# Sixty-four of 512 tokens leave a dense expert product and are gathered by index

## The chip, the cores and the metric

The kernel runs on one core of a Trainium2 chip. The metric is the device time of one execution in microseconds, as a median over runs. The engines are named as in the profile: PE (TensorE), DVE (VectorE), ACT (ScalarE), POOL (GpSimd) and SP (SyncE, which here issues transfers only).

## The reference

A two-layer backbone over 256 latent and 256 context tokens of 1024 features. Each layer has a mixer and then a PEER block, a mixture of 16384 tiny experts of which every token uses 8 heads x 16 = 128. Layer 0 computes the block for all 512 tokens, layer 1 for the 256 latent ones. The change concerns the block alone:

```python
def peer_ffn(x, wq, keys, U, V):
    q = (x @ wq).reshape(B, L, PEER_HEADS, 2, PEER_QDIM // 2)
    s = jnp.einsum('blhpd,hpnd->blhpn', q, keys).astype(F32)
    ...                      # top 16 of each half, top 16 of their sums
    idx = e1 * N_KEYS + e2   # 128 experts of a token
    gate = jax.nn.softmax(top_s, axis=-1).astype(x.dtype)
    ...
        act = jax.nn.gelu(jnp.einsum('tkd,td->tk', U[it], xt), approximate=False) * gt
        return jnp.einsum('tk,tkd->td', act, V[it])
```

## The kernel before

The kernel computes the block densely: the activation of every expert for every token, a gate that is zero for the experts that a token did not choose, and the product with all of V. The 16384 experts are walked in 128 turns `m` of 128 experts, twice for each layer.

In the first walk (`first_products`) a turn is one product of a tile of U with all tokens: 8 chunks of the features, and for each chunk three matmuls, because a float32 value is split in a high and a low part of a narrower type (high x high, high x low, low x high). ScalarE makes the high part of the weights (`high`, w_hi), VectorE the low part (`low`, w_lo), both three turns ahead, in rings of 4; ScalarE applies the gelu, and the activations are stored to HBM (`acts_out`, one plane of 128 experts x tokens for each turn). In the same turns VectorE finds each token's experts and gates (`routing`, in slices, up to turn 53), and from turn 54 on one oct a turn (8 tokens) is turned into a dense table of gates: VectorE writes one-hot rows (`onehots`), TensorE multiplies them (`gates`, 24 small matmuls at line 828, two turns later), ScalarE stages them, and GpSimd's queue stores groups of 32 tokens to HBM (`gates_out`). With 64 octs the last one is multiplied in turn 119.

In the second walk (`second_products`) a turn is: SP loads a tile of V (512 KB), the activations of the turn (`z_load`, 256 KB) and every eighth turn a block of gates (2 MB); VectorE multiplies activation by gate (`gated`, two turns ahead), ScalarE makes the high part (`gate_high`), VectorE the low part (`gate_low`, one turn ahead); TensorE multiplies, again 8 x 3 matmuls, and adds all 128 turns up in the eight PSUM banks, one bank of 512 columns (tokens) for each 128 features. Each engine works its list strictly in order. VectorE's list is:

```python
                for m in range(NKEY):
                    if m + 2 < NKEY:
                        gated(l, m + 2)
                    if m + 1 < NKEY:
                        gate_low(l, m + 1)
                    if m + AHEAD < NKEY:
                        low(l, NKEY + m + AHEAD)
```

`high` of a turn waits until TensorE is done with the turn whose ring slot it takes, `low` waits for `high`, and SP's load of the next V tile waits for `low`. GpSimd does nothing in this walk; its queue holds the constants at the start, the stores of gates, the masks of layer 1 and the keys. Lines 555 and 876 are the matmuls of the first and the second walk, 752 those of the queries, 807 plain float32 matmuls of 128x128, 1205 `high`, 1214 `gate_high`, 1731 `low`, 1756 `gated`, 1762 `gate_low`.

Of the kernel before, what the change touches and what calls it, by code (L numbers as in the profile page):

```python
# [20 lines left out]
U32 = mybir.dt.uint32  # L21
# [4 lines left out]
P = 128  # L26
# [96 lines left out]

WIDTH = (T, SEQ)
TILES = (TT, CHUNKS)
U_BANK = (0, 1, 6, 7)
V_ORDER = (2, 3, 4, 5, 0, 1, 6, 7)

# [16 lines left out]


def octs(l):
    return WIDTH[l] // OCT


def groups(l):
    return WIDTH[l] // GTOK


EXP_TURN = [{slice_turn(l, i, AT_DIFF) + 2: i for i in range(TILES[l])} for l in range(2)]
# [24 lines left out]
def build(nc, a, out):  # L180
    with ExitStack() as ctx:
# [133 lines left out]
        I16 = iota[:, 0:TOPK]  # L315


        def weight_parts(name, hi, lo, ring):
            return [over(name + x, at, ring * TILE)[:, :].rearrange("p (r k n) -> p r k n", r=ring, k=KD)
                    for x, at in (("_w_hi", hi), ("_w_lo", lo))]  # L320
# [18 lines left out]
        def high_part(k, c, width):  # L339
# [42 lines left out]
            ck_exp ck_ready ck_t ck_in cs_ready cs_taken  # L382
            lk_exp lk_ready lk_t lk_in ls_ready ls_done
            qi_exp qi_ready lv_diff lv_exp lv_ready lv_prod lv_taken
            oi_ready osq_ready ors_ready oms_ready ostd_ready mx_ready
            f_in f_added f_tab f_normtaken dve_step lb_diff lb_exp""".split()
        S = {n: sem(n) for n in names}
        w_loaded = [sem(f"w_loaded{r}") for r in range(RING)]
        z_out = [sem(f"z_out{r}") for r in range(ZRING)]
        z_in = [sem(f"z_in{r}") for r in range(ZRING)]  # L390
        gates_out = [nc.dram_tensor(f"gates{l}", (groups(l), P, NKEY, GTOK), F32).ap() for l in range(2)]
        acts_out = [nc.dram_tensor(f"acts{l}", (NKEY, P, WIDTH[l]), F32).ap() for l in range(2)]
        block = ctx.enter_context(nc.Block())

        def parts(hi, lo, x_hi, x_lo):
# [19 lines left out]
        def _(sp):  # L415
# [40 lines left out]
            def z_load(l, m):  # L456

                r = m % ZRING
                wait(sp, S["act_ready"], l * NKEY + m - ZRING + 1)
                sp.dma_start(ZIN[:, r, 0:WIDTH[l]], acts_out[l][m]).then_inc(z_in[r], 16)  # L460

            def gates_block(l, x):

# [4 lines left out]
            def first_products(l, u, v):  # L468

                n0 = AT_PEER[l]  # L470
                for k in range(RING):
                    load(n0 + k, u[k])
                for m in range(NKEY + ZRING):
                    if m < NKEY:
                        k = m + RING
                        load(n0 + k, u[k] if k < NKEY else v[k - NKEY])
                    if l == 0 and m in LATE_TURN:
                        late(LATE_TURN[m])
                    if m == NKEY:
                        for x in range(ZRING - 1):  # L480
                            sp.wait_ge(z_out[x], 16 * (NKEY // ZRING * l + 1))
                            z_load(l, x)
                        for b in range(2):
                            sp.wait_ge(S[f"g_stored{b}"], 16 * sum(groups(x) // 2 for x in range(l + 1)))
                        for x in range(2):
                            gates_block(l, x)
                    if m >= ZRING:
                        z = m - ZRING
                        sp.wait_ge(S["gelu_done"], l * NKEY + z + 1)
                        sp.dma_start(acts_out[l][z], ZOUT[:, z % ZRING, 0:WIDTH[l]]).then_inc(z_out[z % ZRING], 16)  # L490
                for r in range(ZRING):
                    sp.wait_ge(z_out[r], 16 * (NKEY // ZRING * (l + 1)))
# [32 lines left out]
        @block.gpsimd  # L525
        def _(pool):
            for dst, src in first:
                pool.dma_start(dst, src).then_inc(S["consts_in"], 16)

            pool.wait_ge(S["w_used"], used(AT_ABOUT + N_OUT - 1))  # L530
            pool.dma_start(arena[:, 8192:10240], a["keys0"]).then_inc(S["keys_in"], 16)


            def stores(l):

                for g in range(groups(l)):
                    b = g % 2
                    pool.wait_ge(S["g_high"], 2 * l * octs(0) + 8 * (g + 1))
                    pool.dma_start(gates_out[l][g].rearrange("p e t -> p (e t)"), STG[:, b].rearrange("p e t -> p (e t)"))\
                        .then_inc(S[f"g_stored{b}"], 16)  # L540

            stores(0)
            pool.wait_ge(S["ck_exp"], 1)
            pool.dma_start(arena[:, 30752:31776], a["masks"]).then_inc(S["masks_in"], 16)
            pool.wait_ge(S["w_used"], used(AT_HGOUT + N_OUT - 1))
            pool.dma_start(arena[:, 8192:10240], a["keys1"]).then_inc(S["keys_in"], 16)
            stores(1)


        @block.tensor  # L550
        def _(pe):
# [301 lines left out]

            def value_sum(l, c):

                return ps[:, c, :] if l == 0 else ps[:, 2 + c // 2, c % 2 * SEQ:(c % 2 + 1) * SEQ]

            def second_products(l):

                n0, m0, width = AT_PEER[l] + NKEY, l * NKEY, WIDTH[l]  # L860
                pe.wait_ge(S["g_high"], 2 * sum(octs(x) for x in range(l + 1)))
                pe.wait_ge(S["slots_in"], sum(TILES[:l + 1]))
                if l == 0:
                    pe.wait_ge(S["ada_taken"], 3)

                for m in range(NKEY):
                    pe.wait_ge(S["w_used"], used(n0 + m))
                    pe.wait_ge(S["act_ready"], m0 + m + 1)
                    r, z = m % 4, m % ZRING
                    for c in V_ORDER if l == 0 and m == 0 else range(KD):  # L870
                        if m == 0 and l == 0 and c in U_BANK:
                            pe.wait_ge(S["gelu_done"], m0 + NKEY - 3 + U_BANK.index(c))
                        for n, (w, x) in enumerate(parts(WHI[:, r, c, :], WLO[:, r, c, :],
                                                         ACH[:, z, 0:width], ACL[:, z, 0:width])):

                            ins = pe.matmul(value_sum(l, c), w, x, start=m == 0 and n == 0 and (l == 0 or c % 2 == 0),  # L876
                                            stop=m == NKEY - 1 and n == 2, skip_group_check=True)
                        if m == NKEY - 1 and (l == 0 or c % 2 == 1) and c < KD - 1:
                            ins.then_inc(S["sum_done"], 1)
                    ins.then_inc(S["part_used"], 1)  # L880
# [135 lines left out]
        def _(act):  # L1016
# [169 lines left out]
            def gates_staged(l, n):  # L1186

                g, o = n // 4, l * octs(0) + n
                if n % 4 == 0:
                    wait(act, S[f"g_stored{g % 2}"], 16 * (l * groups(0) // 2 + g // 2))  # L1190
                for h in range(2):
                    act.wait_ge(S["oh_used"], 2 * o + h + 1)
                    t0 = n % 4 * OCT + 4 * h
                    copy(STG[:, g % 2, :, t0:t0 + 4], ps[:, 2 + h, :].rearrange("p (t e) -> p e t", t=4))\
                        .then_inc(S["g_high"], 1)
# [11 lines left out]

            def gate_high(l, m):

                width, r = WIDTH[l], m % ZRING  # L1210
                act.wait_ge(S["mul_ready"], l * NKEY + m + 1)
                if m >= ZRING:
                    act.wait_ge(S["part_used"], l * N_PEER + NKEY + m - ZRING + 1)
# [169 lines left out]
        def _(dve):  # L1383
# [262 lines left out]
            def routing(l, i):  # L1646
# [21 lines left out]
                for q in range(2):  # L1668
# [11 lines left out]
                step.done(dve.reciprocal(GSUM[:, 1], GSUM[:, 0]))  # L1680
                tt(GATE[:, 0], GATE[:, 0], wide(GSUM[:, 1].unsqueeze(2), [P, NH, TOPK]), ALU.mult)\
                    .then_inc(S["gates_ready"], 1)
                yield

            def routes(l):
                for i in range(TILES[l]):
                    for _ in routing(l, i):
                        yield

            def key_numbers():  # L1690
                step.done(dve.tensor_copy(KEYNUM, iota[:, :].unsqueeze(2).to_broadcast([P, P, 2])))

            def onehots(l, n):

                o, i = l * octs(0) + n, n * OCT // P
                if n * OCT % P == 0:
                    dve.wait_ge(S["slots_in"], l * TT + i + 1)
                    t = slice(i * P, (i + 1) * P)
                    dve.tensor_copy(KEY1[:, t], SL[:, 1, t])
# [3 lines left out]
                    step.done(tt(GREST, SL[:, 0, t], GHI[:, t], ALU.subtract))  # L1703
                    step.done(dve.tensor_copy(GMID[:, t], GREST))
                    step.done(tt(GLO[:, t], GREST, GMID[:, t], ALU.subtract))
                toks = slice(n * OCT, (n + 1) * OCT)

                def spread(x):
                    return x[:, toks].rearrange("p (v w) -> p v w", w=2).unsqueeze(2).to_broadcast([P, OCT // 2, NKEY, 2])
# [38 lines left out]

            def gated(l, m):

                r, b, width = m % ZRING, m // BLK % 2, WIDTH[l]
                dve.wait_ge(z_in[r], 16 * (NKEY // ZRING * l + m // ZRING + 1))
                if m % BLK == 0:
                    dve.wait_ge(S[f"g_in{b}"], 16 * (NKEY // (2 * BLK) * l + m // (2 * BLK) + 1))
# [2 lines left out]

            def gate_low(l, m):

                r, width = m % ZRING, WIDTH[l]  # L1760
                dve.wait_ge(S["acthi_ready"], l * NKEY + m + 1)
                tt(ACL[:, r, 0:width], ZIN[:, r, 0:width], ACH[:, r, 0:width], ALU.subtract)\  # L1762
                    .then_inc(S["act_ready"], 1)

            def second_products(l):
# [5 lines left out]
                for m in range(NKEY):  # L1771
# [3 lines left out]
                        gate_low(l, m + 1)  # L1775
                    if m + AHEAD < NKEY:
                        low(l, NKEY + m + AHEAD)

            def peer_residual(l):
                def ready(c):  # L1780
# [165 lines left out]
            for n in range(4, 8):  # L1946
# [131 lines left out]
```

## Time and profile before

| what | value |
|---|---|
| median of 3 runs | 3341.94 us (3341.54 to 3345.03) |
| profiled execution, span of its instructions | 3342.5 us |
| PE busy | 3169.0 us (95%) |
| DVE busy | 1942.5 us (58%) |
| ACT busy | 1222.9 us (37%) |
| POOL busy | 20.0 us (1%) |
| layer 0, second walk | from 1357 us |
| layer 1, second walk | 2941 to 3327 us |

Only the span is shown for the profiled execution, so it serves as its time. Busy time of PE counts a matmul from its first to its modelled last moment, and neighbours overlap: the mean duration of a matmul is therefore longer than the step from one to the next, and steps are read from pieces with a count (time by number) or from starts that repeat.

### The profile page before, as it was taken

The page shows a single profiled execution, that of the slowest core. Times are in us where ns is not written, and L with a number is a line of the kernel's source. Part 1 is how long each engine was busy: PE and PEld are TensorE (multiplying, and loading weights), DVE is VectorE, ACT ScalarE, POOL GpSimd, SP SyncE. Part 2 cuts the span into 40 slices and gives each one's busy share as a digit, 9 for nine tenths or more (in the row PEclk, how much of TensorE's full clock was granted, in tenths as well). Part 3 has the DMA queues.
Part 4 walks back from the last instruction along what each step waited for, and adds up shares of the span by engine and source line. Part 5 has one row for each costly group of instructions (what it writes and reads, how often), then busy time and mean ns, then how long its engine had stood idle before and what let it go on. Part 6 is the DMA issues. An engine that isn't in the chain of part 4 may idle for free.

```text
span 3342.5 us, 48135 instructions
## 1 busy us (share of the span) xinstructions
PE 3169.0 (95%) x19664; PEld 2696.4 (81%) x19664; DVE 1942.5 (58%) x3476; ACT 1222.9 (37%) x1871; POOL 20.0 (1%) x41
## 2 busy tenths in 40 slices
PE   7997889999999999999999998997789999999998
PEld 3664478888888888888888886896689999999998
DVE  5347335998555564444444444436839987656665
ACT  3313233333333333333333334325235444544444
POOL 0000000000000000000000000000000000000000
PEclk9998999999999999999999999998999999999999
DMA  5510223445666556765565552322346777787774
GB/s 204 205 60 1 73 85 98 143 144 153 229 236 221 189 189 199 240 198 195 193 199 193 193 176 70 111 76 92 116 159 200 210 254 256 252 274 260 264 262 165
DMA packets 232610, 587.91 MB, mean 176 GB/s; under 512 B 20983, under 2 KB 104008, under 8 KB 228744
## 3 DMA queue, kind: packets, MB, share of 16 engines
q1 hardware_dynamic: 227280, 528.57, 48.7%
q0 software_dynamic: 4208, 53.27, 4.1%
q8 instruction: 156, 2.56, 0.3%
q10 hardware_dynamic: 904, 3.01, 0.3%
q14 instruction: 62, 0.51, 0.0%
HBM read 483.06 MB, written 101.71 MB: 175 GB/s over the span
## 4 chain that ended last, share of the span: by engine, by line
PE 78%; DVE 14%; ACT 4%; issue 2%; DMA 1%; ACTq 0%; SPq 0%; DVEq 0%
PE ps L555 32%; PE ps L876 26%; PE ps L752 10%; PE ps L828 4%; DVE w_lo L1731 3%; PE ps L788 2%; ACT w_hi L1205 2%; PE ps L635 1%; PE ps L600 1%; DVE arena L1638 1%; DVE arena L1756 1%; DVE arena L1632 1%; PE ps L807 1%; DMA arena<-acts 1%; ACT a_t L1072 1%
## 5 line engine op out<-in xcount | busy, mean ns | idle before, releaser
L1731 DVE TENSOR_TENSOR w_lo<-wring,w_hi 128x1024 fp32r<-128x1024 f32 x512 | 626.4, 1224 | 695.3 <-ACT w_hi L1205 693.1
L555 PE MATMUL ps<-a_hi,w_hi 128*128 128x512 f32 (+1 forms) x2048 | 699.8, 342 | 9.4 <-DVE w_lo L1731 5.5
L876 PE MATMUL ps<-act_hi,w_hi 128*128 128x512 f32 (+1 forms) x2048 | 697.7, 341 | 5.2 <-DVE act_lo L1762 5.2
L555 PE MATMUL ps<-a_hi,w_lo 128*128 128x512 f32 (+1 forms) x2048 | 688.6, 336 | 0.0
L876 PE MATMUL ps<-act_lo,w_hi 128*128 128x512 f32 (+1 forms) x2048 | 688.3, 336 | 0.0
L555 PE MATMUL ps<-a_lo_q,w_hi 128*128 128x512 f32 (+1 forms) x2048 | 688.2, 336 | 0.0
L876 PE MATMUL ps<-act_hi,w_lo 128*128 128x512 f32 (+1 forms) x2048 | 687.8, 336 | 0.0
L1205 ACT CAST w_hi<-wring 128x1024 fp32r<-128x1024 f32 x512 | 533.8, 1043 | 227.7 <-PE ps L876 227.7
L555 PEld LDWEIGHTS ps<-a_hi,w_hi 128*128 128x128 f32 x2048 | 388.3, 190 | 57.0 <-DVE w_lo L1731 8.2
L876 PEld LDWEIGHTS ps<-act_hi,w_hi 128*128 128x128 f32 x2048 | 387.9, 189 | 52.7 <-issue 5.9
L555 PEld LDWEIGHTS ps<-a_hi,w_lo 128*128 128x128 f32 x2048 | 388.4, 190 | 41.0
L876 PEld LDWEIGHTS ps<-act_lo,w_hi 128*128 128x128 f32 x2048 | 388.6, 190 | 39.8
L876 PEld LDWEIGHTS ps<-act_hi,w_lo 128*128 128x128 f32 x2048 | 388.5, 190 | 39.9
L555 PEld LDWEIGHTS ps<-a_lo_q,w_hi 128*128 128x128 f32 x2048 | 388.8, 190 | 38.1
L1233 ACT ACTIVATE arena<-ps 128x512 f32<-128x512 f32 (+1 forms) x256 | 125.9, 492 | 754.4 <-PE ps L555 696.7
L1214 ACT CAST act_hi<-arena 128x512 fp32r<-128x512 f32 (+1 forms) x256 | 131.7, 515 | 456.2 <-DVE arena L1756 456.2
L1714 DVE TENSOR_TENSOR second_onehot<-key_numbers,slot_keys 128x1024 bf16<-128x1024 bf16 x96 | 66.2, 690 | 188.7 <-PE ps L828 188.7
L828 PE MATMUL ps<-gated_onehot,second_onehot 128*128 128x128 bf16 x2304 | 149.2, 219 | 0.0
L1756 DVE TENSOR_TENSOR arena<-arena 128x512 f32<-128x512 f32 (+1 forms) x256 | 141.2, 552 | 11.6 <-DMA arena<-acts 9.3
L828 PEld LDWEIGHTS ps<-gated_onehot,second_onehot 128*128 128x128 bf16 x2304 | 132.5, 97 | 18.1 <-issue 16.7
L1762 DVE TENSOR_TENSOR act_lo<-arena,act_hi 128x512 fp32r<-128x512 f32 (+1 forms) x256 | 141.4, 552 | 0.4
L555 PE MATMUL ps<-arena 128*128 128x256 f32 (+4 forms) x372 | 102.7, 427 | 12.8 <-DVE arena L1557 9.5
(253 smaller groups left out, 3448.5 us busy)
## 6 DMA issues: line engine op xcount, KB each, us to landing
wring<-in_u SPq DMA_DIRECT2D x256, 512.0 KB, 4.0
wring<-in_v SPq DMA_DIRECT2D x256, 512.0 KB, 3.7
gates<-arena POOLq DMA_DIRECT2D x24, 2048.0 KB, 8.6
wring<-in_ada SPq DMA_DIRECT2D x64, 512.0 KB, 5.5
acts<-arena SPq DMA_DIRECT2D x128, 256.0 KB, 4.4
arena<-acts SPq DMA_DIRECT2D x128, 256.0 KB, 3.4
arena<-gates SPq DMA_DIRECT2D x16, 2048.0 KB, 11.2
wring<-in_hgin SPq DMA_DIRECT2D x40, 512.0 KB, 3.4
```

The source lines that it names most:

```text
L555: ins = pe.matmul(o, l, r, start=n == 0, stop=n == len(pairs) - 1, **kw)
L752: ins = pe.matmul(o, w, x, start=c == 0 and n == 0, stop=c == KD - 1 and n == 2)
L788: ins = pe.matmul(mixed(l, c), W[:, n % RING, k, :], src[:, k, :], start=k == 0 and (l == 0 or c % 2 == 0), stop=k == KD - 1, skip_group_c ...
L828: ins = pe.matmul(ps[:, 2 + h, u * NKEY:(u + 1) * NKEY], OHB[:, n % 2, 2 * h + u // 2, :, u % 2], OHA[:, n % 2, x, 2 * h + u // 2, :, u % ...
L876: ins = pe.matmul(value_sum(l, c), w, x, start=m == 0 and n == 0 and (l == 0 or c % 2 == 0), stop=m == NKEY - 1 and n == 2, skip_group_che ...
L1205: copy(WHI[:, k % 4].rearrange("p k n -> p (k n)"), wring[:, n % RING * TILE:(n % RING + 1) * TILE])\
L1214: copy(ACH[:, r, 0:width], ZIN[:, r, 0:width]).then_inc(S["acthi_ready"], 1)
L1233: act.activation(ZOUT[:, m % ZRING, 0:WIDTH[l]], ps[:, U_BANK[m % 4], 0:WIDTH[l]], ACT.Gelu)\
L1714: tt(OHB[:, n % 2], numbers, spread(KEY2), ALU.is_equal)
L1731: tt(WLO[:, k % 4].rearrange("p k n -> p (k n)"), wring[:, n % RING * TILE:(n % RING + 1) * TILE], WHI[:, k % 4].rearrange("p k n -> p (k ...
L1756: tt(z, z, RB[l][:, b, :, m % BLK, :], ALU.mult).then_inc(S["mul_ready"], 1)
L1762: tt(ACL[:, r, 0:width], ZIN[:, r, 0:width], ACH[:, r, 0:width], ALU.subtract)\
```

## The change

For layer 0, the first 64 tokens (`PICK`) leave the second walk: its matmuls are 448 columns wide (`DENSE`), and the gates of these tokens are no longer made into a dense table, so there are 56 octs and 14 groups. The first walk still computes activations for all 512 tokens. For the 64 tokens, after the first tile's routing VectorE writes the numbers of each token's 128 experts, the addresses of their activations in `acts_out`, and the gates (`slot_numbers`), and GpSimd's queue spreads them so that a partition holds one token and one half of its 128 slots (`spread_slots`). After the first walk GpSimd fetches, for each of 64 slots k, 128 rows of V by index (`v_row`, one row of 4 KB in each partition, a ring of 4) and 128 activations by index (`words`, 4 bytes in each partition, in four batches of 16). VectorE multiplies a batch of activations with its gates and adds row times activation to an accumulator (`row_added`), one row in 1.66 turns, from turn 10 to turn 114. In turn 122 TensorE adds the accumulator, transposed and with the two halves of a token summed, into the 64 free columns of each PSUM bank (`fold`).

```diff
+PICK = (64, 0)
+DENSE = tuple(w - p for w, p in zip(WIDTH, PICK))
+SPREAD = P // PICK[0]
+QUARTER = PICK[0] // 4
+VRING = 4
+ADD_FIRST = 10
...
 def octs(l):
-    return WIDTH[l] // OCT
+    return DENSE[l] // OCT
 def groups(l):
-    return WIDTH[l] // GTOK
+    return DENSE[l] // GTOK
+def stored(l, b):
+    return sum((groups(x) + 1 - b) // 2 for x in range(l))
+def add_turn(k):
+    return ADD_FIRST + (NKEY - ADD_FIRST - 12) * k // PICK[0]
+ADD_TURN = [[k for k in range(PICK[0]) if add_turn(k) == m] for m in range(NKEY)]
+FOLD_TURN = NKEY - 6
+def pool_order():
+    first = [(oct_turn(0, 4 * g + 3) + OCT_TURNS[0] + 3, 0, g) for g in range(groups(0))]
+    return sorted(first + [(slice_turn(0, 0, SLICES - 1) + 1, 1, 0)])
...
+        VROW = [arena[:, at:at + D] for at in range(28672, 28672 + VRING * D, D)]
+        VACC = arena[:, 34560:34560 + D]
+        PSTG = hand[:, 0:3 * P].rearrange("p (q k) -> p q k", q=3)
+        PSLOT = PSTG if SPREAD == 1 else view(33920, "p (q k) -> p q k", q=3, k=PICK[0])
+        PACT = arena[:, 34112:34112 + PICK[0]]
+        FOLD = ident[:, :] if SPREAD == 1 else arena[:, 34240:34240 + PICK[0]]
+        PNUM = hand[:, 3 * P:3 * P + 1]
+        v_rows = a["v0"].rearrange("a b d -> (a b) d")
...
+        act_cells = acts_out[0].rearrange("a p t -> (a p t)").unsqueeze(1)
...
-                sp.dma_start(ZIN[:, r, 0:WIDTH[l]], acts_out[l][m]).then_inc(z_in[r], 16)
+                sp.dma_start(ZIN[:, r, 0:DENSE[l]], acts_out[l][m, :, PICK[l]:WIDTH[l]]).then_inc(z_in[r], 16)
...
-            stores(0)
+            def store(l, g):
+                b = g % 2
+                pool.wait_ge(S["g_high"], 2 * l * octs(0) + 8 * (g + 1))
+                pool.dma_start(gates_out[l][g].rearrange("p e t -> p (e t)"), STG[:, b].rearrange("p e t -> p (e t)"))\
+                    .then_inc(S[f"g_stored{b}"], 16)
+            def spread_slots():
+                n = PICK[0]
+                pool.wait_ge(S["pick_ready"], 1)
+                if SPREAD > 1:
+                    for r in range(SPREAD):
+                        pool.dma_start(PSLOT[r * n:(r + 1) * n], PSTG[0:n, :, r * n:(r + 1) * n]).then_inc(S["pick_in"], 16)
+                    pool.wait_ge(S["pick_in"], 16 * SPREAD)
+            def fetch(dst, table, q, k, sem):
+                pool.indirect_dma_start(dst, None, table, bass.IndirectOffsetOnAxis(
+                    ap=PSLOT[:, q, k:k + 1].bitcast(U32), axis=0)).then_inc(sem, 16)
+            def v_row(k):
+                wait(pool, S["row_added"], k - VRING + 1)
+                fetch(VROW[k % VRING], v_rows, 0, k, v_row_in[k % VRING])
+            def words(q):
+                for k in range(q * QUARTER, (q + 1) * QUARTER):
+                    fetch(PACT[:, k:k + 1], act_cells, 1, k, S[f"act_in{q}"])
+            def picked_rows():
+                pool.wait_ge(S["part_used"], NKEY)
+                for k in range(2):
+                    v_row(k)
+                for r in range(ZRING):
+                    pool.wait_ge(z_out[r], 16 * (NKEY // ZRING))
+                words(0)
+                for k in range(2, PICK[0]):
+                    if k % QUARTER == QUARTER // 2 and k // QUARTER < 3:
+                        words(k // QUARTER + 1)
+                    v_row(k)
+            for _, kind, g in pool_order():
+                if kind:
+                    spread_slots()
+                else:
+                    store(0, g)
+            picked_rows()
...
-                return ps[:, c, :] if l == 0 else ps[:, 2 + c // 2, c % 2 * SEQ:(c % 2 + 1) * SEQ]
+                return ps[:, c, PICK[0]:T] if l == 0 else ps[:, 2 + c // 2, c % 2 * SEQ:(c % 2 + 1) * SEQ]
+            def fold():
+                pe.wait_ge(S["fold_ready"], 1)
+                pe.wait_ge(S["row_added"], PICK[0])
+                for c in range(KD):
+                    pe.matmul(ps[:, c, 0:PICK[0]], VACC[:, c * P:(c + 1) * P], FOLD, start=False, stop=True,
+                              skip_group_check=True)
             def second_products(l):
-                n0, m0, width = AT_PEER[l] + NKEY, l * NKEY, WIDTH[l]
+                n0, m0, width = AT_PEER[l] + NKEY, l * NKEY, DENSE[l]
...
+                    if l == 0 and m == FOLD_TURN:
+                        fold()
...
-                width, r = WIDTH[l], m % ZRING
+                width, r = DENSE[l], m % ZRING
...
+                if l == 0 and i == 0:
+                    slot_numbers()
                 yield
+            def slot_numbers():
+                flat = GATE.rearrange("p q h k -> p q (h k)")
+                dve.wait_ge(S["gates_ready"], 1)
+                dve.tensor_copy(PSTG[:, 2], flat[:, 0])
+                step.done(stt(PSTG[:, 1], flat[:, 1], float(NKEY), flat[:, 2], ALU.mult, ALU.add))
+                dve.tensor_copy(PSTG[:, 0].bitcast(U32), PSTG[:, 1])
+                step.done(ts(PSTG[:, 1], PSTG[:, 1], float(T), PNUM, ALU.mult, ALU.add))
+                dve.tensor_copy(PSTG[:, 1].bitcast(U32), PSTG[:, 1]).then_inc(S["pick_ready"], 1)
...
+            def fold_matrix():
+                if SPREAD > 1:
+                    dve.tensor_reduce(FOLD, ident[:, :].rearrange("p (r t) -> p t r", r=SPREAD), AXX, ALU.add)
+                step.done(tt(PSTG[:, 0], ident[:, :], iota[:, :], ALU.mult))
+                dve.tensor_reduce(PNUM, PSTG[:, 0], AXX, ALU.add).then_inc(S["fold_ready"], 1)
+                dve.wait_ge(S["fold_ready"], 1)
+            def row_added(k):
+                if k % QUARTER == 0:
+                    q = slice(k, k + QUARTER)
+                    dve.wait_ge(S[f"act_in{k // QUARTER}"], 16 * QUARTER)
+                    step.done(tt(PACT[:, q], PACT[:, q], PSLOT[:, 2, q], ALU.mult))
+                dve.wait_ge(v_row_in[k % VRING], 16 * (k // VRING + 1))
+                if k == 0:
+                    ts(VACC, VROW[0], PACT[:, 0:1], None, ALU.mult).then_inc(S["row_added"], 1)
+                else:
+                    dve.wait_ge(S["row_added"], k)
+                    stt(VACC, VROW[k % VRING], PACT[:, k:k + 1], VACC, ALU.mult, ALU.add).then_inc(S["row_added"], 1)
...
-                o, i = l * octs(0) + n, n * OCT // P
-                if n * OCT % P == 0:
+                o, t0 = l * octs(0) + n, PICK[l] + n * OCT
+                i = t0 // P
+                if n == 0 or t0 % P == 0:
...
+                    if l == 0:
+                        for k in ADD_TURN[m]:
+                            row_added(k)
...
             query_weights(0)
+            fold_matrix()
             first_products(0)
```

## Rows read from the trace of the kernel before

**Rows 1.** The profile's page, part 1: busy time, share of the span and instructions by engine
```profile
PE 3169.0 (95%) x19664; PEld 2696.4 (81%) x19664; DVE 1942.5 (58%) x3476; ACT 1222.9 (37%) x1871; POOL 20.0 (1%) x41
```

**Rows 2.** Windows, both value stages: us, engine busy (instructions), PEclk, DMA share, GB/s
```profile
1500.00:1700.00 200.00, 200.00 (x884) 165.68 (x883) 89.62 (x111) 60.89 (x74) 0.00 (x0) 1.00 0.59 192
...
2941.00:3327.00 386.00, 383.68 (x3072) 376.23 (x3073) 240.87 (x384) 171.95 (x257) 0.00 (x0) 1.00 0.75 249
```

**Rows 3.** Waits, DVE alone, layer 0 value stage: total us, times, longest us
```profile
DVE w_lo L1731 <- ACT w_hi L1205: 369.8, 125, 3.3
DVE arena L1756 <- DMA arena<-acts: 3.8, 1, 3.8
```

**Rows 4.** Chain that ended last, 1290 to 1420 us: start us, us, what
```profile
1298.21 1.40 PE ps L828 x24
1299.61 5.54 PE ps L555 x24
...
1313.47 43.62 PE ps L555 x192
1357.09 63.01 PE ps L876 x278
```

**Rows 5.** One line (L1205), 1500 to 1560 us: durations, first and last start
```profile
L1205 ACT CAST w_hi<-wring x11: 1048/1048/1048, 1504.1 to 1558.5; 128x1024 fp32r<-128x1024 f32 x11
```

**Rows 6.** Chain that ended last, whole span: three long pieces and one repeated
```profile
455.55 65.54 PE ps L752 x288
521.84 14.54 PE ps L807 x128
...
2466.30 34.80 PE ps L752 x288
...
2699.26 5.80 PE ps L555 x48
```

**Rows 7.** Timeline around 1700 us, ACT and DVE of one turn: start us, us, what
```profile
1699.90 1.05 ACT L1205 CAST w_hi<-wring 128x1024 fp32r<-128x1024 f32 x1 [1.88 <-PE ps L876]
...
1700.98 1.23 DVE L1731 TENSOR_TENSOR w_lo<-wring,w_hi 128x1024 fp32r<-128x1024 f32 x1 [3.01 <-ACT w_hi L1205]
...
1702.12 0.69 DVE L1756 TENSOR_TENSOR arena<-arena 128x512 f32<-128x512 f32 x1
...
1702.73 0.69 DVE L1762 TENSOR_TENSOR act_lo<-arena,act_hi 128x512 fp32r<-128x512 f32 x1
```

**Rows 8.** Groups by line and shape, DVE: busy us, mean ns
```profile
L1563 DVE SCALAR_TENSOR_TENSOR arena<-arena,dskip,ps 128x512 f32<-128x512 f32 x8 | 6.0, 747 | 23.0 <-PE ps L555 23.0
```

**Rows 9.** Groups by line and shape, POOL: busy us, mean ns
```profile
L539 POOL DMA_DIRECT2D gates<-arena x24 | 12.8, 532 | 1373.2 <-ACT arena L1194 1373.2
L528 POOL DMA_DIRECT2D ident<-in_ident x1 | 0.7, 678 | 0.8 <-POOLq L2070 0.8
...
L528 POOL DMA_DIRECT2D ong<-in_ong x1 | 0.5, 534 | 0.0
...
L2070 POOL MEMSET const-float32-1.0<- 128x1 f32 x1 | 0.1, 99 | 0.0
```

**Rows 10.** DMA issues, whole span: KB each, median us from issue to landing
```profile
acts<-arena SPq DMA_DIRECT2D x128, 256.0 KB, 4.4
...
ident<-in_ident POOLq DMA_DIRECT2D x1, 64.0 KB, 4.5
...
ong<-in_ong POOLq DMA_DIRECT2D x1, 0.5 KB, 9.2
```

**Rows 11.** DMA, layer 0 value stage: packets; issues as in rows 10
```profile
DMA packets 65719, 130.37 MB, mean 189 GB/s; under 512 B 4321, under 2 KB 32993, under 8 KB 65685
...
q1 hardware_dynamic: 65685, 129.89, 57.2%
...
arena<-acts SPq DMA_DIRECT2D x125, 256.0 KB, 3.3
arena<-gates SPq DMA_DIRECT2D x14, 2048.0 KB, 11.2
```

More of the change, by code:

```diff
@@ L384, in build @@
             qi_exp qi_ready lv_diff lv_exp lv_ready lv_prod lv_taken
+            pnum_ready pick_ready pick_in act_in0 act_in1 act_in2 act_in3 pick_act row_added fold_ready
             oi_ready osq_ready ors_ready oms_ready ostd_ready mx_ready
@@ L390, in build @@
         z_in = [sem(f"z_in{r}") for r in range(ZRING)]
+        v_row_in = [sem(f"v_row_in{r}") for r in range(VRING)]
         gates_out = [nc.dram_tensor(f"gates{l}", (groups(l), P, NKEY, GTOK), F32).ap() for l in range(2)]
         acts_out = [nc.dram_tensor(f"acts{l}", (NKEY, P, WIDTH[l]), F32).ap() for l in range(2)]
+        act_cells = acts_out[0].rearrange("a p t -> (a p t)").unsqueeze(1)
         block = ctx.enter_context(nc.Block())
@@ L483, in first_products @@
                         for b in range(2):
-                            sp.wait_ge(S[f"g_stored{b}"], 16 * sum(groups(x) // 2 for x in range(l + 1)))
+                            sp.wait_ge(S[f"g_stored{b}"], 16 * stored(l + 1, b))
                         for x in range(2):
@@ L531, in _ @@
             pool.dma_start(arena[:, 8192:10240], a["keys0"]).then_inc(S["keys_in"], 16)
[L534 to L540, printed above, removed]
-            stores(0)
+            def store(l, g):
[3 more added lines that the diff above has]
+                    .then_inc(S[f"g_stored{b}"], 16)
@@ L546, in _ @@
             pool.dma_start(arena[:, 8192:10240], a["keys1"]).then_inc(S["keys_in"], 16)
-            stores(1)
+            for g in range(groups(1)):
+                store(1, g)
         @block.tensor
@@ L1189, in gates_staged @@
                 if n % 4 == 0:
-                    wait(act, S[f"g_stored{g % 2}"], 16 * (l * groups(0) // 2 + g // 2))
+                    wait(act, S[f"g_stored{g % 2}"], 16 * (stored(l, g % 2) + g // 2))
                 for h in range(2):
@@ L1705, in onehots @@
                     step.done(tt(GLO[:, t], GREST, GMID[:, t], ALU.subtract))
-                toks = slice(n * OCT, (n + 1) * OCT)
+                toks = slice(t0, t0 + OCT)
                 def spread(x):
@@ L1749, in gated @@
             def gated(l, m):
-                r, b, width = m % ZRING, m // BLK % 2, WIDTH[l]
+                r, b, width = m % ZRING, m // BLK % 2, DENSE[l]
                 dve.wait_ge(z_in[r], 16 * (NKEY // ZRING * l + m // ZRING + 1))
@@ L1758, in gate_low @@
             def gate_low(l, m):
-                r, width = m % ZRING, WIDTH[l]
+                r, width = m % ZRING, DENSE[l]
                 dve.wait_ge(S["acthi_ready"], l * NKEY + m + 1)
```

## Prediction

> **What bounds the kernel now.** The first view is the page's busy time: TensorE is busy in 95% of the span, VectorE in 58%, GpSimd in 1% [rows 1]. The share is a mean over stages, so the windows come next, for the stage that the change cuts, layer 0's value product: TensorE is busy in all of 200 us out of 200, VectorE in 90 us, ScalarE in 61, at the full granted clock (1.00, the 2.4 GHz level) [rows 2]. The waits of that stage say the same from the other side: VectorE waits 370 us in 125 turns for ScalarE's `w_hi` and 3.8 us in all for a DMA [rows 3], and `w_hi` waits for TensorE (the chain runs over TensorE alone from 1357 us on) [rows 4]. The stage is as long as its 3072 matmuls: ScalarE starts `w_hi` 11 times between 1504.1 and 1558.5 us, so a turn of 24 matmuls takes 54.4 / 10 = 5.44 us, 226.7 ns a matmul [rows 5].
>
> **The sum is made against** the profiled execution, 3342.5 us from first to last instruction, the only time shown for it; the three runs without a profile have the median 3341.94, 0.6 us away, so nothing is added. A difference under 0.2% (6.7 us) is what a measurement here can't tell from none.
>
> **Narrower products (448 columns for 512).** The trace has the same kind of matmul at two widths. 288 of them take 65.54 us with 512 columns and 34.80 us with 256 [rows 6]: 30.74 us / 288 / 256 = 0.417 ns a column, one column per cycle at 2.4 GHz, on top of a constant 14 ns. 64 columns fewer are 26.7 ns, so 200.0 ns a matmul and 4.80 us a turn; 3072 x 26.7 = **82 us** removed. Bounds: if all of 226.7 ns went with the width, 87 us; by the layer 1 pieces of 48 matmuls in 5.80 us (120.8 ns) against 226.7, 81 us [rows 5, 6]. Weight loads don't set a floor at 200 ns, because the same 128x128 loads keep up with a matmul each 120.8 ns.
>
> **Eight octs fewer.** 64 tokens less are 8 octs of gates less in the stage before (turns 112 to 119). There the chain alternates 5.54 us of product with 1.40 us of gates, and the last eight turns, without gates, take 43.62 / 8 = 5.45 us [rows 4]: 6.94 - 5.45 = 1.49 us, times 8 = **11.9 us** removed. The onehots, copies, shorter gate stores and narrower `gated`, `gate_high` and `gate_low` go too, but they hide under TensorE and count nothing.
>
> **Added on TensorE:** the fold, 8 matmuls of 128x128 by 64 columns. Plain 128x128 ones take 14.54 us / 128 = 0.11 us [rows 6]; at most 0.9 us together. It stands in turn 122 and the last row is added in turn 114, 38 us earlier.
>
> **Added on VectorE, hidden or not.** One row add is `scalar_tensor_tensor` over 1024 elements. The 512 wide one takes 0.747 us [rows 8]; 512 more cost 1.23 - 0.69 = 0.54 by the subtractions of both widths [rows 7]: 1.29 us (doubled outright, 1.49). 64 adds are 83 us, in a stage where VectorE is idle more than half of the time. What counts is the place. In the turn shown, TensorE's turn begins where ScalarE starts `w_hi` (1699.90), VectorE ends `gate_low` at 1703.42, and this activation is multiplied two turns later [rows 7]. With an add in between and turns of 4.80 us the spare is 9.6 - 3.5 - 1.3 = 4.8 us. So adds that find their row landed cost nothing, and a row late by x costs x - 4.8. `slot_numbers` and `fold_matrix` are a few short instructions: the second stands while TensorE makes queries, the first in turn 13 with weights three turns ahead; both zero, at most 1 to 2 us if that cover went.
>
> **Added on GpSimd: 128 indirect fetches,** 64 of value rows (512 KB) and 64 of activation words (128 words of 4 bytes). The trace has none, so call one fetch's time on GpSimd's queue t. Below: a direct transfer of 128 partitions is issued in 0.53 us whatever its size [rows 9]. Next: ten constants issued back to back land 4.5 (first) to 9.2 us (last) after their issue [rows 10], so the last lands 9 x 0.534 + 4.7 = 9.5 us after the first, 1.06 us each, and issue doesn't wait for landing. Above: each waits for its own landing, 4.5 us. A fetch differs from these by reading 128 indices; I take 1.1 to 1.5 us, near the rows of the same queue and partitions.
>
> How much may it be? The ring has 4 rows, and rows 8, 24 and 40 stand behind a batch of 16 word fetches that GpSimd reaches when row 3, 19 or 35 is added, 9, 8 and 9 turns before the row is due. In that go row 7's fetch, 16 words and row 8's (18t) and a landing (5 us, between 4.5 and 9.2): 18t + 5 against 9 x 4.80 - 1.3 + 4.8 = 46.7 us (8 turns: 41.9). The first batch starts some 6 us into the stage (two row fetches, then the last activations' store, 4.4 us [rows 10]) and is due in turn 10: 6 + 16t + 5 against 48 + 2.3 + 4.8 = 55.1. So **fetches are free up to t = 2.0 us** (1.8 with a landing of 9.2); past it the four stalls add to about 70t - 164 us. At 1.5 nothing; I count 0.
>
> The SBUF — State Buffer page of the Trainium skill (Who interferes with whom) says that a VectorE instruction with two SBUF inputs and a GpSimd instruction that reads SBUF shut each other out. No row here shows it; by it a fetch could wait out an add, by my estimate up to 1.3 us: t of 2.4 to 2.8 and a sum 4 to 32 us worse.
>
> **Transfers.** The stage moves 129.9 MB in 57.2% of the engines' 691 us, 48.7 engine-us a MB and 96 ns a packet [rows 11]. After: 7.8 MB less of activations and gates, 33.6 MB of rows, 8192 words at a packet each: 156 x 48.7 + 790 = 8390 engine-us, 524 of the new stage's 615 us, 85%. Layer 1's value stage runs at 75% with 99% of its time on TensorE [rows 2], and activations land in 3.3 us [rows 11] where the order of loads, three turns ahead, allows 3 x 4.80 - 1.3 = 13. I count 0, and keep some 10 us for the range.
>
> **Sum:** 3342.5 - 82.0 - 11.9 + 0.9 = 3249.5, say **3250 us**; its own range 3244 to 3260.
>
> **Rivals.**
> 1. *Fetches cost 2 to 3.6 us, since reading indices is slow or waits out adds, or the engines at 85% land them late.* The word batches then stall VectorE in turn 10 and before rows 8, 24 and 40; at 3 us 70 x 3 - 164 = 46 us come back: 3296, and between 3260 and 3335. For it: nothing shows an indirect fetch. Against: 1.06 us each in rows 9 and 10.
> 2. *Slower: GpSimd's queue becomes the bound.* From t = 3.7 us on the stalls eat the 93 us. At 4.5 us, the landing of one transfer [rows 10], 151 us come back: 3400. Against: ten transfers were issued 0.53 us apart while none had landed.
> 3. *Slower by far: GpSimd reads each index by itself.* At the shortest instruction that the trace has on it, 0.10 us [rows 9], 128 indices are 12.8 us a fetch and 128 fetches 1638 us against a stage of 615: with 11 us of start and landing and 14 turns (67 us) behind the last row, 3250 + 1101 = 4351. Against: a direct transfer, whose 128 partitions are addressed too, takes 0.53 us. The GPSIMD Engine Reference of the Trainium skill (Performance pitfalls for Q7 kernels) speaks for it: some 102 cycles for each small read command, one per gather index its example, and its Specifications give 1.2 GHz; 128 of them would be an estimated 10.9 us, and the time some 4110.
> 4. *The width gives nothing,* a floor under the matmuls at 227 ns: 3342.5 - 11.9 + 0.9 = 3332. Against it are the 120.8 ns at 256 columns.
>
> **How the numbers follow.** Forecast 0.60; rival 1 0.16; rival 2 0.13; rival 3 0.05; rival 4 0.03; and 0.03 where stall and gain meet within 0.2%. Faster is forecast, 1 and 4: 0.79; same 0.03; slower 0.18. The time is the forecast's; the range runs from the full 87 us (3244) to where rivals 1 and 4 end (3335), which holds 0.79.
>
> **What the next profile would show.** Right: `act_hi`/`w_hi` matmuls of 448 columns at a turn of 4.80 us (`w_hi` starts), the value stage at some 615 us, eight more plain turns of 5.45 us before it, VectorE's waits on row and word fetches with nothing behind them on TensorE, GpSimd's fetches at 1 to 2 us. Wrong: TensorE idle behind `act_lo` in turns 10 and around 23, 49 and 76 (rivals 1 and 2); idle in every turn (3); turns of 5.44 us (4).

## The result, and the profile after

The changed kernel takes 3264.73 us (median of 4 runs, 3264.47 to 3273.93) for 3341.9 (4 runs, 3341.54 to 3345.03): ratio 0.9773, 95% interval 0.9759 to 0.9787, **77 us faster**. The range held it, but only because it was drawn out to 3335 for rivals 1 and 4: the forecast of 3250 was 15 us too low, the forecast's own range (to 3260) missed by 5, and by the time alone it would be taken for rival 1 (3260 to 3335). The rows below show neither rival. The execution with the profile is the slowest of each four, by 9 us after and by 3 before; spans are compared with each other: 3342.5 to 3272.1, 70.4 us less.

The page and the windows answer to [rows 1, 2]. TensorE's share is what it was; in the value stage VectorE now works 121 us of 200, GpSimd 54, the transfer engines 79%, and TensorE is busy in all of it, at the full granted clock (1.00).

```profile
PE 3096.9 (95%) x19488; PEld 2688.0 (82%) x19488; DVE 1979.8 (61%) x3512; ACT 1207.7 (37%) x1855; POOL 159.5 (5%) x169
```

```profile
1500.00:1700.00 200.00, 200.00 (x970) 181.76 (x969) 121.00 (x146) 65.23 (x81) 54.00 (x50) 1.00 0.79 262
```

The chain (for [rows 4]; start us, us, what) is still TensorE's, and it shows three small things that are new:

```profile
1258.96 87.15 PE ps L638 x384
...
1349.32 6.41 DMA arena<-acts
...
1355.75 0.63 DVE arena L1883
1356.38 0.55 DVE act_lo L1889
...
1357.06 595.43 PE ps L969 x2880
1952.49 1.73 PE ps L946 x16
1954.22 25.00 PE ps L969 x123
...
1979.24 5.97 DVE h_t L1714 x15
```

Sixteen plain turns take 87.15 us (5.45 each) where eight had gates before. The value stage then starts at 1346.1 instead of 1357.1 us. Its first activations land late (6.41 us), TensorE loses 1.2 us there, and the fold takes 1.73 us. From 1346.1 to VectorE's first residual at 1979.2 the stage takes 633.1 us, where it took 691.6. Up to the fold a matmul takes 595.43 / 2880 = 206.7 ns, behind it 25.00 / 123 = 203 ns.

The turn (for [rows 5]; ScalarE's `w_hi`, first and last start of ten) is 44.7 / 9 = 4.97 us, 4.96 by the other turns, so 206.7 ns a matmul; the forecast had 4.80:

```profile
L1298 ACT CAST w_hi<-wring x10: 1052/1053/1053, 1600.4 to 1645.1; 128x1024 fp32r<-128x1024 f32 x10
```

The fetches, which no row before showed (groups by line on POOL: busy us, mean ns | idle before), and the DMA of the stage with their landing (for [rows 11]; packets, MB, share of the engines; then median us to landing):

```profile
L593 POOL DMA_INDIRECT arena<-acts,arena x64 | 71.0, 1109 | 20.1 <-issue 19.2 <-DMA acts<-arena 0.9
L593 POOL DMA_INDIRECT arena<-in_v,arena x64 | 68.2, 1065 | 462.9 <-DVE arena L1814 347.4 <-PE ps L638 85.4 <-DVE arena L1811 26.3
```

```profile
q1 hardware_dynamic: 61996, 121.93, 58.0%
q0 software_dynamic: 11264, 33.60, 17.2%
...
arena<-in_v,arena POOLq DMA_INDIRECT x64, 6.1
arena<-acts,arena POOLq DMA_INDIRECT x64, 4.3
```

The stage's waits (total us, times, longest us), VectorE's and then TensorE's, and the row adds' durations. VectorE waits for no row and no batch of words, and TensorE waits once:

```profile
DVE w_lo L1858 <- ACT w_hi L1298: 254.7, 126, 4.4
DVE h_t L1714 <- PE ps L969: 11.0, 1, 11.0
DVE arena L1883 <- DMA arena<-acts: 6.4, 1, 6.4
```

```profile
PE ps L969 <- DVE act_lo L1889: 1.2, 1, 1.2
```

```profile
L1814 DVE SCALAR_TENSOR_TENSOR arena<-arena x63: 1275/1279/1285, 1404.3 to 1915.1; 128x1024 f32<-128x1024 f32 x63
```

### The profile page after: what moved, and what is told of

Read it like the earlier page. It is cut to its first block, busy times and chain, and to the rows that moved or that the text cites. A ratio compares the mean times of both kernels' runs of the same rounds, so it can differ in the third digit from the quotient of the medians.

```text
span 3272.1 us, 47990 instructions
## 1 busy us (share of the span) xinstructions
PE 3096.9 (95%) x19488; PEld 2688.0 (82%) x19488; DVE 1979.8 (61%) x3512; ACT 1207.7 (37%) x1855; POOL 159.5 (5%) x169
## 4 chain that ended last, share of the span: by engine, by line
PE 84%; DVE 11%; ACT 2%; DMA 1%; issue 1%; ACTq 0%; SPq 0%; DVEq 0%
PE ps L638 33%; PE ps L969 30%; PE ps L835 10%; PE ps L911 4%; PE ps L871 2%; DVE w_lo L1858 1%; PE ps L718 1%; PE ps L683 1%; DVE arena L1731 1%; DVE arena L1725 1%; PE ps L890 1%; PE ps L708 1%; ACT a_t L1165 1%; DVE arena L2022 1%; DVE arena L1733 0%
## 5 line engine op out<-in xcount | busy, mean ns | idle before, releaser
L969 PE MATMUL ps<-act_hi,w_hi 128*128 128x448 f32 (+1 forms) x2048 | 676.2, 330 | 5.3 <-DVE act_lo L1889 5.3
L969 PE MATMUL ps<-act_lo,w_hi 128*128 128x448 f32 (+1 forms) x2048 | 666.9, 326 | 0.0
L969 PE MATMUL ps<-act_hi,w_lo 128*128 128x448 f32 (+1 forms) x2048 | 666.4, 325 | 0.0
L1307 ACT CAST act_hi<-arena 128x448 fp32r<-128x448 f32 (+1 forms) x256 | 124.7, 487 | 524.4 <-DVE arena L1883 524.4
L1883 DVE TENSOR_TENSOR arena<-arena 128x448 f32<-128x448 f32 (+1 forms) x256 | 132.8, 519 | 11.5 <-DMA arena<-acts 10.4
L911 PE MATMUL ps<-gated_onehot,second_onehot 128*128 128x128 bf16 x2112 | 136.8, 219 | 0.0
L911 PEld LDWEIGHTS ps<-gated_onehot,second_onehot 128*128 128x128 bf16 x2112 | 121.5, 97 | 16.0 <-issue 14.7
L1889 DVE TENSOR_TENSOR act_lo<-arena,act_hi 128x448 fp32r<-128x448 f32 (+1 forms) x256 | 132.9, 519 | 0.5
```

The costliest lines, as they stand in the source:

```text
L911: ins = pe.matmul(ps[:, 2 + h, u * NKEY:(u + 1) * NKEY], OHB[:, n % 2, 2 * h + u // 2, :, u % 2], OHA[:, n % 2, x, 2 * h + u // 2, :, u % ...
L1307: copy(ACH[:, r, 0:width], ZIN[:, r, 0:width]).then_inc(S["acthi_ready"], 1)
L1883: tt(z, z, RB[l][:, b, :, m % BLK, :], ALU.mult).then_inc(S["mul_ready"], 1)
```

## The experiments

**1. Is it the width or the traffic?** The value stage gave back 58.5 us, not 81. The turn is 0.16 us longer than the line through 256 and 512 columns says. Either a matmul of 448 columns costs that by itself, or rows, words and adds slow it. The kernel before, with other columns in each 16 turns:

```diff
+COLUMNS = ((0, 512), (64, 512), (0, 448), (0, 512), (0, 384), (128, 512), (32, 512), (0, 512))
...
+                    a0, a1 = columns_of(l, m)
...
-                            ins = pe.matmul(value_sum(l, c), w, x,
+                            ins = pe.matmul(value_sum(l, c)[:, a0:a1], w, x,
```

> The kernel before, with no fetch and no row add; only the columns that the second walk of layer 0 multiplies change every 16 turns: 512; 448 from column 64; 448 from column 0; 512; 384 from 0; 384 from 128; 480 from 32; 512. It leaves out the products of the tokens outside these columns in those turns. Read from it: the step between ScalarE's w_hi starts, which is the length of a turn of 24 matmuls. Theory A (the width or the place of 448 columns costs 6.7 ns a matmul more than the line through 256 and 512 columns): 4.96 us for 448 from 64; if it is the place, 4.80 for 448 from 0, if it is the count, 4.96 there too. Theory B (the fetched rows, words and adds slow the matmuls down): 4.80 us for both. By the line alone: 5.44 for 512, 5.12 for 480, 4.16 for 384.

One execution, 3277.57 us. The starts of `w_hi` over 16 turns each: 448 from column 64, 448 from 0, 384 from 0, 480 from 32:

```profile
L1211 ACT CAST w_hi<-wring x17: 1046/1050/1053, 1442.1 to 1519.9; 128x1024 fp32r<-128x1024 f32 x17
...
L1211 ACT CAST w_hi<-wring x17: 1047/1050/1053, 1519.9 to 1597.8; 128x1024 fp32r<-128x1024 f32 x17
...
L1211 ACT CAST w_hi<-wring x17: 1052/1054/1054, 1684.8 to 1751.4; 128x1024 fp32r<-128x1024 f32 x17
...
L1211 ACT CAST w_hi<-wring x17: 1047/1051/1051, 1818.0 to 1902.5; 128x1024 fp32r<-128x1024 f32 x17
```

77.8, 77.9, 66.6 and 84.5 us over 16 turns: 4.86, 4.87, 4.16 and 5.28 us. The place makes no difference, and 384 is on the line. 448 is 0.06 to 0.07 us above it and 480 0.16 without any fetch or add. So the width costs something by itself, but at 448 in this run less than the 0.16 us of the changed kernel.

**2. The changed kernel without rows.** The other side of the same question:

```diff
-            picked_rows()
...
-                    if l == 0:
-                        for k in ADD_TURN[m]:
-                            row_added(k)
+                    if l == 0 and m == ADD_FIRST:
+                        dve.memset(VACC, 0.0).then_inc(S["row_added"], PICK[0])
```

> The changed kernel without its 128 fetches and 64 row adds (the accumulator is set to zero, so the 64 tokens get no value sum in layer 0; the gates' octs, the width of 448 and the fold stay). Theory A (the width itself costs 206.7 ns): turns stay at 4.96 us and the time at 3262 to 3265 us. Theory B (the traffic of rows and words slows the matmuls): turns of 4.80 us, 128 x 0.16 = 20 us less, about 3244.

Measured: 3260.82 us (3259.76 to 3261.40), ratio 0.9757 (0.9741 to 0.9774) to the kernel before. **With all 128 fetches, 64 adds and 33.6 MB the changed kernel's median is only 4 us higher** (3264.73). Theory B falls. Theory A doesn't hold as put either: the turn is 58.4 / 12 = 4.87 us, as in experiment 1, neither 4.80 nor 4.96:

```profile
L1297 ACT CAST w_hi<-wring x13: 1047/1050/1053, 1499.9 to 1558.3; 128x1024 fp32r<-128x1024 f32 x13
```

**3. What if a fetch cost three times as much?** This tests the sum that set the bound of free fetches.

```diff
-                    fetch(PACT[:, k:k + 1], act_cells, 1, k, S[f"act_in{q}"])
+                    for at in (34112, 34176, 34304):
+                        fetch(arena[:, at + k:at + k + 1], act_cells, 1, k, S[f"act_in{q}"])
...
-                    dve.wait_ge(S[f"act_in{k // QUARTER}"], 16 * QUARTER)
+                    dve.wait_ge(S[f"act_in{k // QUARTER}"], 3 * 16 * QUARTER)
```

> Each word fetch is issued three times (the two copies go to unused columns), so that a batch takes 48 x 1.40 = 67 us of GpSimd's queue for 22. The forecast's stall sum: from row 7's fetch to the add of row 8 there are 43 us, and 4.8 us of spare; 1.1 + 67 + 1.3 + 6 us of landing are 75.6, so VectorE and TensorE lose 28, 33 and 28 us at rows 8, 24 and 40 and 17 us in turn 10, 105 in all: about 3370 us, slower than before. Rival (the batches are hidden by more than the ring of four, or TensorE has more spare): 3265 to 3300.

Measured: 3361.43 us (3358.23 to 3364.26), ratio 1.0057 (1.0040 to 1.0074): 97 us more than the changed kernel, for 105 expected, and 20 us (0.6%) more than the kernel before. VectorE's waits (total us, times, longest) and TensorE's show the four stalls where the sum put them, one for words and three for rows:

```profile
DVE arena L1815 <- DMA arena<-in_v,arena: 87.5, 3, 31.5
DVE arena L1809 <- DMA arena<-acts,arena: 18.6, 1, 18.6
```

```profile
PE ps L970 <- DVE act_lo L1890: 87.2, 5, 26.7
```

VectorE waits 18.6, 28.2, 31.5 and 27.8 us, and TensorE then stands still for 13.5, 23.3, 26.7 and 23.0, each time 4.8 to 5.1 us less. That difference is the spare, forecast as 4.8 us. For TensorE the sum had 17, 28, 33 and 28, so it was 4 to 6 us too long at each stall: from row 7's fetch to row 8's add 69.7 us went by, not 75.6. The same trace tells something of the turn. In 13 starts before the last stall it is 58.4 / 12 = 4.87 us, in 13 after it 59.5 / 12 = 4.96:

```profile
L1299 ACT CAST w_hi<-wring x13: 1047/1050/1053, 1693.1 to 1751.5; 128x1024 fp32r<-128x1024 f32 x13
...
L1299 ACT CAST w_hi<-wring x13: 1053/1053/1053, 1900.3 to 1959.8; 128x1024 fp32r<-128x1024 f32 x13
```

Rows are fetched and added on both sides, so the traffic does not make the difference: the 448-column product has two paces in one execution. In the changed kernel's trace the pace changes too, at the fold. What sets it is open.

**4. Twice the adds.**

```diff
+                stt(arena[:, 10240:10240 + D], VROW[k % VRING], PACT[:, k:k + 1], VROW[k % VRING], ALU.mult, ALU.add)
                 if k == 0:
                     ts(VACC, VROW[0], PACT[:, 0:1], None, ALU.mult).then_inc(S["row_added"], 1)
```

> Every row add is preceded by a second one of the same size into an unused tile: 64 x 1.28 = 82 us more on VectorE. Forecast's theory (VectorE's adds stand in 4.8 us of spare): no change, 3265 us within 3. Rival (VectorE's order is close to the path, so that adds cost what they take): up to 3347.

Measured: 3264.18 us (3263.49 to 3272.61), ratio 0.9766 (0.9750 to 0.9782): no change against the changed kernel for 82 us more of VectorE. The timeline of a turn with the two adds shows their place in the order: `w_lo`, two adds, `gated`, ScalarE's `act_hi`, and only then the next `w_hi`:

```profile
1599.76 1.23 DVE L1859 TENSOR_TENSOR w_lo<-wring,w_hi 128x1024 fp32r<-128x1024 f32 x1 [1.10 <-ACT w_hi L1298]
...
1600.90 1.28 DVE L1810 SCALAR_TENSOR_TENSOR arena<-arena 128x1024 f32<-128x1024 f32 x1
...
1602.10 1.28 DVE L1815 SCALAR_TENSOR_TENSOR arena<-arena 128x1024 f32<-128x1024 f32 x1
...
1603.29 0.62 DVE L1884 TENSOR_TENSOR arena<-arena 128x448 f32<-128x448 f32 x1
...
1603.95 0.57 ACT L1307 CAST act_hi<-arena 128x448 fp32r<-128x448 f32 x1 [4.22 <-DVE arena L1884]
...
1604.42 1.04 ACT L1298 CAST w_hi<-wring 128x1024 fp32r<-128x1024 f32 x1
```

From `w_hi` to `w_hi` such turns take 5.75 us and those without an add 3.39; TensorE, three turns of weights behind, goes on at 4.96.

**5. Which widths are on the line?** As in experiment 1, with other widths from column 0:

```diff
+COLUMNS = ((0, 512), (0, 496), (0, 464), (0, 440), (0, 432), (0, 416), (0, 400), (0, 352))
```

> The kernel before without fetches and adds, and with other widths from column 0 in the second walk of layer 0, 16 turns each: 512, 496, 464, 440, 432, 416, 400, 352; it leaves out the other tokens' products in those turns. Theory 1 (the line through 256, 384 and 512 columns, 0.417 ns a column and 14 ns, holds outside one spot at 448 to 480): turns of 5.44, 5.28, 4.96, 4.72, 4.64, 4.48, 4.32 and 3.84 us. Theory 2 (a step is rounded up to some grain, so that 512 and 384 are lucky): steps come in plateaus, the same turn for neighbouring widths, up to 0.16 us above the line.

One execution, 3259.49 us. Turns by the usual step between `w_hi` starts, with those of experiment 1, beside the line through 256 and 512 columns, 24 x (13.3 + 0.417 x columns) ns, which gives 4.80 us at 448:

| columns | 512 | 496 | 480 | 464 | 448 | 440 | 432 | 416 | 400 | 384 | 352 |
|---|---|---|---|---|---|---|---|---|---|---|---|
| turn, us | 5.44 | 5.28 | 5.28 | 5.04 | 4.87 | 4.80 | 4.70 | 4.48 | 4.32 | 4.16 | 3.87 |
| above the line, us | 0 | 0 | 0.16 | 0.08 | 0.07 | 0.08 | 0.06 | 0 | 0 | 0 | 0.03 |

Neither theory as put: the spot is wide, 432 to 480 columns, where the line's step lies between 193 and 213 ns, just above the 188 to 192 ns that one weight load takes in the traces. At 416 (187 ns) and below, but for 0.03 us at 352, and at 496 (220 ns) and above the line holds. Each load starts with the matmul before its own. At 448 columns (changed kernel, first two lines) it ends some 20 ns before its own matmul starts, at 384 (experiment 1) some 20 ns after:

```profile
1600.17 0.19 PEld L969 LDWEIGHTS ps<-act_lo,w_hi 128*128 128x128 f32 x1
...
1600.38 0.37 PE L969 MATMUL ps<-act_lo,w_hi 128*128 128x448 f32 x1
...
1700.03 0.19 PEld L882 LDWEIGHTS ps<-act_hi,w_hi 128*128 128x128 f32 x1
...
1700.20 0.33 PE L882 MATMUL ps<-act_hi,w_hi 128*128 128x384 f32 x1
```

So the spot lies just above the width at which the step becomes as long as the load. That the weight load is the reason is not shown: no run here changed it.

**6. Half the tokens.**

```diff
-PICK = (64, 0)
+PICK = (32, 0)
```

> The changed kernel with 32 tokens picked for 64: 480 columns, 32 rows in eight words a batch, 60 octs. By the forecast's line (213.3 ns at 480): 3342 - 41 - 6 + 2 = 3297 us. By the step of 220.0 ns measured at 480 columns: 3072 x 6.7 = 20.5 us, so 3342 - 20.5 - 6 + 2 = 3317 us.

Measured: 3312.35 us (3308.14 to 3313.33), ratio 0.9909 (0.9892 to 0.9925). The time is nearer to the sum by the measured step than to that by the line, but neither step came: the turn was 5.20 us (216.7 ns) here, 5.28 (220.0) in experiment 1 and 5.12 (213.3) by the line. So 480 columns have two paces as well.

**7. Twice the tokens.** 384 columns are on the line. Do GpSimd, VectorE and the transfers carry 128 rows?

```diff
-PICK = (64, 0)
+PICK = (128, 0)
-VRING = 4
+VRING = 7
...
+                for k in range(QUARTER):
+                    word(k)
                 for k in range(2, PICK[0]):
-                    if k % QUARTER == QUARTER // 2 and k // QUARTER < 3:
-                        words(k // QUARTER + 1)
+                    if k - 2 + QUARTER < PICK[0]:
+                        word(k - 2 + QUARTER)
                     v_row(k)
```

> The changed kernel with 128 tokens picked: 384 columns, 128 rows and words, 48 octs, a ring of 7 rows, and a word fetch before each row fetch after the first 32. Theory 1 (TensorE stays the bound, the step at 384 columns is 173.3 ns, GpSimd at 2 x 1.4 us and VectorE at 2.5 + 1.1 us fit in a turn of 4.16 us): 3342 - 164 - 24 + 3 = about 3157 us. Theory 2 (the transfer engines become the bound: 64 tokens took them from 62% to 79% of a stage of about 620 us, so 116 us; 128 tokens need about 375 + 232 = 607 us of them in a stage of 532): stage 610 to 670 us, time 3230 to 3290 us, with TensorE waiting for VectorE and VectorE for rows or activations.

Measured: 3224.23 us (3223.14 to 3224.85), ratio 0.9649 (0.9633 to 0.9665). The time and the stage (1335 to 1926 us, 591) lie below theory 2 and far above theory 1, and the reason is neither. The transfer engines' share is 0.96, but VectorE waits 1.0 us in all for rows and words. The timeline shows a loop between ScalarE and VectorE that leaves TensorE out: `w_hi` ends, `w_lo`, the add, `gated`, `act_hi`, the next `w_hi`, 4.42 us from `w_hi` to `w_hi` where TensorE needs 4.16; turns with two adds take 5.81. The window row says what TensorE loses by it:

```profile
1595.21 1.04 ACT L1298 CAST w_hi<-wring 128x1024 fp32r<-128x1024 f32 x1
...
1596.29 1.23 DVE L1858 TENSOR_TENSOR w_lo<-wring,w_hi 128x1024 fp32r<-128x1024 f32 x1 [1.06 <-ACT w_hi L1298]
...
1597.43 1.28 DVE L1814 SCALAR_TENSOR_TENSOR arena<-arena 128x1024 f32<-128x1024 f32 x1
...
1598.62 0.55 DVE L1883 TENSOR_TENSOR arena<-arena 128x384 f32<-128x384 f32 x1
...
1599.21 0.52 ACT L1307 CAST act_hi<-arena 128x384 fp32r<-128x384 f32 x1 [2.96 <-DVE arena L1883]
...
1599.63 1.04 ACT L1298 CAST w_hi<-wring 128x1024 fp32r<-128x1024 f32 x1
```

```profile
1400.00:1800.00 400.00, 373.15 (x2032) 349.01 (x2031) 307.89 (x360) 124.28 (x170) 231.83 (x197) 1.00 0.96 336
```

**8. The adds out of the loop.** ScalarE makes `w_hi` while VectorE adds:

```diff
                     if m + 1 < NKEY:
                         gate_low(l, m + 1)
+                    if l == 0:
+                        for k in ADD_TURN[m]:
+                            row_added(k)
                     if m + AHEAD < NKEY:
                         low(l, NKEY + m + AHEAD)
-                    if l == 0:
-                        for k in ADD_TURN[m]:
-                            row_added(k)
```

> The kernel with 128 picked tokens, and in VectorE's list the row adds of a turn stand before low instead of behind it, while ScalarE makes w_hi. Theory 1 (the 128-token kernel is held by a loop between ScalarE and VectorE: w_hi 1.05, w_lo 1.23 less its overlap, the add 1.28, gated 0.55, act_hi 0.51, then the next w_hi, 4.42 us a turn with one add and 5.81 with two): with the adds out of the loop a turn of one add is TensorE's 4.16 us, one with two some 4.8, and the time falls by 30 to 60 us, to 3165 to 3195. Theory 2 (the transfer engines at 94 to 100% are the bound): no change, 3215 to 3225, and the waits go over to row and word fetches or activations.

Measured: **3180.42 us** (3170.81 to 3181.93), ratio 0.9515 (0.9499 to 0.9530): 162 us less than the kernel before and 84 less than the changed one. Theory 1. In the same window TensorE is busy in 396 us of 400 (the profiled execution is the fastest of the four, 3170.81), and the transfers rise from 336 to 376 GB/s, so a share of 0.96 had not been their bound. Now VectorE does wait for them, 43 us in 23 waits over the stage:

```profile
1400.00:1800.00 400.00, 396.23 (x2272) 395.94 (x2272) 343.87 (x405) 144.80 (x190) 286.62 (x211) 0.99 1.02 376
```

```profile
DVE arena L1883 <- DMA arena<-acts: 30.0, 17, 7.1
...
DVE arena L1814 <- DMA arena<-in_v,hand: 8.9, 5, 4.0
DVE arena L1808 <- DMA arena<-acts,hand: 3.9, 1, 3.9
```

## Why the prediction was right, point by point

- **What bounds the stage:** right. TensorE's step sets it, before and after, and what was called hidden stayed hidden: 64 adds (1.279 us each for 1.29 forecast; twice of them cost nothing), the fetches, and `slot_numbers` (the piece of 360 matmuls around turn 13 takes 81.9 us before and after).
- **Narrower products, 82 us: the term that was mis-sized.** The step that failed reads 448 columns off a line through 256 and 512. Both ends are on the line, as are 384 to 416 and 496, but 448 is not: 202.7 or 206.7 ns for 200.0. At 4.96 us a turn 128 turns give 61 us, at 4.87 they give 73. The prediction set a floor by weight loads aside because loads keep up with 120.8 ns at 256 columns; that argument says nothing of the widths between, where the excess lies. What causes it stays open. Apart from it the profiled executions add up: 61.4 - 1.7 (fold) - 1.2 (start) are the 58.5 us of the stage, and with 11.0 before it and 0.9 after it 70.4. That the medians are 77 apart would fit executions without a profile that ran at the faster pace (an estimate: 122 turns of 0.09 us are 11 us, and the profiled one is 9 us slower); their pace can't be read.
- **Eight octs, 11.9 us:** right. The gates' turns that became plain ones save 8 x (6.94 - 5.45); the stage began 11.0 us earlier, since the chain was already 0.9 us late at 522 us, in the queries, ahead of any changed instruction. Experiments 1 and 5, which change nothing up to there, differ by 4 us at that place, so this is scatter between executions.
- **The fold, 0.9 us:** 1.73. A plain float32 matmul leaves two records (16 for 8 here), and the row that priced it counted 128 records of 64 matmuls. A start of 1.2 us, for activations that land 6.4 us after their load beside rows and words, was not foreseen.
- **Fetches, 1.1 to 1.5 us:** right, and decisive. One takes 0.93 to 1.80 us (mean 1.07 for rows, 1.11 for words), 1.40 us apart in a batch. Rival 1 and rival 2 need 2.0 and 3.7 us. Tripling the words made the stalls of rivals 1 and 2 come true at the places that the sum named, and TensorE lost 87 us of the 105 that it gave.
- **The rule of the Trainium skill's page SBUF — State Buffer** (Who interferes with whom) on VectorE's two-tile reads beside GpSimd's: the trace agrees as far as it goes. All 25 fetches with no VectorE instruction beside them take 0.94 or 0.95 us, the 103 others 0.93 to 1.80; the timeline of the first batch shows both in turn:

```profile
1357.50 0.94 POOL L593 DMA_INDIRECT arena<-acts,arena  x1 [0.30 <-issue]
...
1360.31 0.94 POOL L593 DMA_INDIRECT arena<-acts,arena  x1 [0.30 <-issue]
1361.56 1.80 POOL L593 DMA_INDIRECT arena<-acts,arena  x1 [0.31 <-issue]
1363.66 0.94 POOL L593 DMA_INDIRECT arena<-acts,arena  x1 [0.30 <-issue]
1364.90 1.79 POOL L593 DMA_INDIRECT arena<-acts,arena  x1 [0.30 <-issue]
```

  The two of 1.8 us run beside `w_lo`, `gated` and `gate_low`, which read two SBUF tiles each. Every VectorE instruction beside a fetch reads two, so what one with a single SBUF input would do is not shown. The price was counted as up to 1.3 us a fetch and is at most 0.86.
- **Rival 3, one read per index:** not so here; a fetch with 128 indices takes 0.94 us alone, 0.41 more than a direct transfer's 0.53. The price for each gathered index in the Trainium skill's GPSIMD Engine Reference (Performance pitfalls for Q7 kernels) is given there for Q7 kernels and doesn't carry over to these fetches: 10.9 us by it, an estimate, for 0.94 measured.
- **Transfers at 85%:** 58.0 + 17.2 = 75% over the stage (79% in the window of 200 us), and no bound; experiment 8 moved 376 GB/s in the same stage.
- **The spare of 4.8 us** held in experiment 3 (4.8 to 5.1), but it was not the whole of it: ScalarE and VectorE form the loop of experiment 7, whose turn with an add takes 4.42 us there and 4.54 at 448 columns (experiment 3, where they catch up after a stall). At 64 tokens that leaves 0.4 us of air in a turn with an add, and turns without one make up for what runs over, as experiment 4 shows.

## What to carry to other kernels

A price read between two sizes is an interpolation, and the size itself need not lie on the line, as 448 columns did not: measure it, in spare turns of the kernel, before counting on it. An indirect fetch of 128 rows costs GpSimd's queue about as much as two or three direct transfers (1.07 to 1.40 us for 0.53), so here a few tokens of a dense product with sparse gates could move to idle engines at nearly no cost, as long as a batch in the queue is shorter than the time that the ring of fetched rows bridges. When more is moved, look for loops between two helper engines in their list order: one line of order was worth 44 us where bandwidth looked like the bound.

## What the runs showed of the hardware that was not expected

Matmuls with split float32 operands and 432 to 480 columns run 2.5 to 6.7 ns above the line of the other widths, and at 448 and 480 at two paces (202.7 and 206.7 ns, 216.7 and 220.0), which can change within one execution, after a stall or at the fold; the cause is open. The transfer engines' share of 0.96 at 336 GB/s was not their bound: another order of VectorE's list moved 376 GB/s at a share of 1.02.
